# Filler products of ones in TensorE's waits at stage changes and at the end of the setup, inverses awaited in pairs, and a conditioning product placed ahead of the turned rows

## The reference, cut to what matters

```python
for l in range(DEPTH):                                   # DEPTH = 2
    mod = (silu(c) @ w_mod + b_mod).reshape(c.shape[0], 9, 1, 1024)
    h = modulate(rmsnorm(x, norm_w[0]), mod[:, 0], mod[:, 1])
    x = x + 0.5 * mod[:, 2] * swiglu(h, ffn1_w_in, ffn1_w_out)
    h = modulate(rmsnorm(x, norm_w[1]), mod[:, 3], mod[:, 4])
    mix, new = token_mixers(h, ...)                      # SSD, GLA and dilated attention, then w_out
    x = x + mod[:, 5] * mix
    h = modulate(rmsnorm(x, norm_w[2]), mod[:, 6], mod[:, 7])
    x = x + 0.5 * mod[:, 8] * swiglu(h, ffn2_w_in, ffn2_w_out)
y = rmsnorm(x, norm_f)
```

## Time and profile before

| | value |
|---|---|
| median of 3 runs | 2466.9 us (2463.86 to 2469.29) |
| the profiled execution, its time | 2464.18 us |
| its span, first to last instruction | 2461.3 us |
| mean granted TensorE clock | 0.992 |
| PE busy | 2399.5 us, 97% of the span |
| DVE busy | 1630.4 us, 66% |
| ACT busy | 1033.2 us, 42% |

### The profile page before, as it was taken

How to read it: one execution, slowest core, us unless ns; L and a number is a source line. 1 busy time by engine, 2 the same in 40 slices (tenths; PEclk the granted TensorE clock), 3 DMA queues, 4 the chain that set the end, 5 groups by cost and what they waited for, 6 DMA issues and landing times. The chain is left out here.

```text
span 2461.3 us, 48269 instructions
## 1 busy us (share of the span) xinstructions
PE 2399.5 (97%) x18967; PEld 2243.0 (91%) x18967; DVE 1630.4 (66%) x2800; ACT 1033.2 (42%) x1679; POOL 11.4 (0%) x43
## 2 busy tenths in 40 slices
PE   7999999999999999999999999999999999999998
PEld 5998999898977999899999999988999689999997
DVE  7872784565857786288478538736577678846854
ACT  5551452343554554145255315415256445523532
POOL 0000000000000000000000000000000000000000
PEclk8999999999999999999999999999999999999999
DMA  8246335622233224723233553364221431323331
GB/s 303 82 134 223 109 99 187 203 61 74 76 123 96 69 79 136 230 80 96 87 83 86 165 187 103 112 230 133 61 75 51 144 99 52 103 83 89 93 88 62
DMA packets 367530, 285.81 MB, mean 116 GB/s; under 512 B 18273, under 2 KB 355479, under 8 KB 366982
## 3 DMA queue, kind: packets, MB, share of 16 engines
q1 hardware_dynamic: 366956, 283.36, 37.3%
q10 hardware_dynamic: 410, 0.18, 0.0%
HBM read 271.71 MB, written 11.79 MB: 115 GB/s over the span
## 5 line engine op out<-in xcount | busy, mean ns | idle before, releaser
L352 PE MATMUL PS<-f_xH,f_wqH 128*128 128x288 f32 x2140 | 635.5, 297 | 3.1 <-issue 3.0
L352 PE MATMUL PS<-f_xL,f_wqH 128*128 128x288 f32 x2140 | 632.5, 296 | 0.0
L352 PE MATMUL PS<-f_xH,f_wqL 128*128 128x288 f32 x2140 | 630.5, 295 | 0.0
L352 PEld LDWEIGHTS PS<-f_xH,f_wqH 128*128 128x128 f32 x2140 | 401.4, 188 | 6.2 <-issue 5.6
L352 PEld LDWEIGHTS PS<-f_xH,f_wqL 128*128 128x128 f32 x2140 | 403.5, 189 | 0.0
L352 PEld LDWEIGHTS PS<-f_xL,f_wqH 128*128 128x128 f32 x2140 | 402.0, 188 | 0.0
L352 PE MATMUL PS<-f_actH,f_wqH 128*128 128x288 f32 x1408 | 321.5, 300 | 1.3 <-DVE f_wqL L1044 1.3
L352 PE MATMUL PS<-f_actH,f_wqL 128*128 128x288 f32 x1408 | 315.7, 296 | 0.0
L352 PE MATMUL PS<-f_actL,f_wqH 128*128 128x288 f32 x1408 | 315.7, 296 | 0.0
L776 DVE SCALAR_TENSOR_TENSOR xT<-PS,modT,xT 128x288 f32<-128x288 f32 (+1 forms) x80 | 41.4, 517 | 361.6 <-PE PS L352 361.4
L352 PEld LDWEIGHTS PS<-f_actH,f_wqH 128*128 128x128 f32 x1408 | 230.8, 189 | 27.0 <-issue 25.0
(11 more groups left out here) (541 smaller groups left out, 4274.0 us busy)
## 6 DMA issues: line engine op xcount, KB each, us to landing
wslot<-in_ffn_w_in SPq DMA_DIRECT2D x176, 512.0 KB, 5.0
masks<-in_w_mod SPq DMA_DIRECT2D x42, 1536.0 KB, 6.5
wslot<-in_ffn_w_out SPq DMA_DIRECT2D x64, 384.0 KB, 4.2
wslot<-in_w_in SPq DMA_DIRECT2D x48, 512.0 KB, 4.8
wslot<-in_ffn_w_out SPq DMA_DIRECT2D x64, 320.0 KB, 3.4
setup<-in_w_mod SPq DMA_DIRECT2D x6, 1536.0 KB, 12.9
wslot<-in_w_out SPq DMA_DIRECT2D x16, 512.0 KB, 4.6
dec<-in_cache_attn_k SPq DMA_DIRECT2D x16, 384.0 KB, 3.9
```

The lines of the kernel that those rows point to most:

```text
L352: ins = e.matmul(outs[j], w, x_hl[j][part], start=(start and w is wh and part == 0), stop=(stop and w is wl), skip_group_check=True)
```

## The change

Eight edits, all on TensorE's stream. Fillers are products of the constant tile `ones` (128 x 128, float32) with itself, into a PSUM bank that nobody reads; they signal nothing and wait for nothing. They stand: ten behind the last `turn_rows` of the setup; six behind the last down product of each of the four feed-forward blocks; three ahead of the last `values` of each attention part and four at that block's end; five at the end of each output projection. In the output projection `part(2)` waits for two of ACT's four copies and `part(3)` for all four. In the setup `products_of(5)` moves ahead of the turns of groups 0 to 3.

```diff
@@ setup, TensorE
-                for m in range(4):
+                products_of(5)
+                for m in range(5):
                     turn_rows(m)
-                products_of(5)
-                turn_rows(4)
                 turn_rows(5).then_inc(sem("mods_turned"), 1)
+                for _ in range(10):
+                    e.matmul(PS[:, 1, 0:P], ones[:], ones[:], start=True, stop=True)
@@ new helper
+        def warm(e, bank, n):
+            for _ in range(n):
+                e.matmul(PS[:, bank, 0:P], ones[:], ones[:], start=True, stop=True, skip_group_check=True)
@@ ffn_block, TensorE
                             for h in range(2):
                                 for d in range(DT - 2, DT):
                                     last_down(d, h)
+                            warm(e, 1, 6)
@@ input projection and attention, TensorE
+                        if s - 4 == NU - 2:
+                            warm(e, 4, 3)
                         if 0 <= s - 4 < NU and s % 2 == 0:
                             values(s - 4)
                         if 0 <= s - 2 < NU:
                             turn(s - 2)
                         if s == CIN_TURN:
                             turn_cin()
+                    warm(e, 4, 4)
@@ output projection, TensorE
                     spread_inverses()
-                    e.wait_ge(sem("y_spread_kept"), 2 * SG)
                     for d in range(2, 4):
+                        e.wait_ge(sem("y_spread_kept"), 2 * (d - 1))
                         part(d, READY)
@@ end of the output projection, TensorE
                     for h in range(2):
                         for d in range(DT - 2, DT):
                             last_part(d, h)
+                    warm(e, out_bank(4), 5)
```

## The result

The changed kernel takes 2477.15 us at the median of 20 executions (2467.61 to 2484.88), against 2466.49 us for 20 of the kernel before (2461.46 to 2472.39). The ratio is 1.0035, with a 95% interval of 1.0025 to 1.0044. So the change costs 0.35%, 8.6 us by the ratio (10.7 between the two medians), where I had forecast no change.

A forecast was written before the change was run, and what follows sets the result against it. TensorE, busy 97% of the span, was taken as the bound, leaving its pauses, clock and work. Terms 5.2 - 0.3 + 1.6 - 1.8 - 4.6 = +0.1 us, plus 0.4, made 2466.9 + 0.5 = 2467.4 us, range 2462 to 2472.

The forecast's parts named there:

- attention: Attention's end, twice: meeting 0.3 us later, 1.2 us of clock gained; net -0.9 us each, -1.8 in all.
- the inverses: Inverses awaited in pairs, twice: 0.6 us earlier start plus 1.7 us of clock; -2.3 us each, -4.6 in all.
- I take -1.2: Clock gain per layer behind attention's end, where the slow stretch would run at full clock; bounds 0 and -1.6 us.
- so that gives the full 1.7 us: Clock gain per layer behind the inverses: the clock holds after the pause falls from 1.44 to 0.85 us.
- the difference between executions: Whole kernel: in other executions the clock falls at other pauses, so fewer twofold gains; 0.4 us added.
- Feed-forward ends: Four ends, six fillers each ahead of the meeting: +1.31 us each, +5.2 in all, less 0.3 of clock.
- Rival 1: Drain does not wait for the fillers, so the meetings are not held up: 2459 us, chance 0.13.
- The gain of -0.3: Feed-forward ends: full clock at the input projection's opening saves 0.3 us once; bounds 0 and -1.7.
- Setup: Ten fillers at the setup's end cost 2.6 us, a warm first stage returns 1.0, moved product 0: +1.6.
- the bound: Setup: most the first stage could gain from a full clock, -1.9 us, half of its first 3.8 us.
- Output projection's end: Five fillers (1.09 us) end before DVE's last sum: 0, at most +0.1 us.
- rival 2: The clock falls anyway, a little later, behind unshortened real pauses; fillers are paid, little returns: 2474 us, chance 0.13.

The follow-up runs named there:

- e12: The kernel before, unchanged, run again for a second profile: 2468.17 us (12 executions), ratio 1.0000 [0.9989, 1.0011].
- e14: The kernel before, unchanged, run for a third profile: one execution, 2467.62 us.
- e1: The whole change again, against the kernel before: 2477.43 us (8 executions), ratio 1.0035 [1.0022, 1.0048].
- e5: Only the six fillers at each feed-forward end added to the kernel before: 2473.35 us (12 executions), ratio 1.0024 [1.0011, 1.0037].
- e11: Only fillers at each feed-forward end, twelve instead of six, added to the kernel before: 2476.24 us (7 executions), ratio 1.0046 [1.0028, 1.0064].
- e8: Only the fillers at attention's end and the output projection's end added to the kernel before: 2473.11 us (12 executions), ratio 1.0017 [1.0001, 1.0033].
- e9: Only the three and four fillers at attention's end added to the kernel before: 2470.33 us (12 executions), ratio 1.0010 [0.9999, 1.0022].
- e15: Only attention's fillers added to the kernel before, run again for a second profile: one execution, 2461.41 us.

## Why the prediction was wrong

**The parts add up.** By the ratios of the parts run alone: feed-forward ends +5.9, setup +1.2, attention +2.5, output end +0.2, pairs -2.0; together +7.8 us, against +8.6 for the whole. Each part is known to 2 or 3 us, so their sum to some 6: it calls for no hidden interaction, and can't exclude a small one. A second sum, from the traces, comes to the same: four ends of 1.31, the setup's 2.7 less 0.5, twice 0.53 at attention's end, and nothing gained in the state-space stages in the mean, +8.5. My terms were +4.9, +1.6, -1.8, 0 and -4.6 (of which the pairs are all of the last). The miss therefore lies mostly in two terms: attention, off by 4.3 us, and the inverses, off by 2.6.

**The step that failed** is the gain of clock in these two, "I take -1.2" and "so that gives the full 1.7 us". The mechanism was seen right in the profile after: both pauses shrank (that at the inverses to 0.86 us, for 0.85 worked out), the clock held at both places, and the stages took 131.0 and 131.1 us against 133.3 and 133.7, which is -2.3 and -2.6, where I had -1.2 - 2.3 = -3.5 in each. Over all profiles of the two kernels it is 134.5 against 134.5: of the 7 us forecast for the two stages nothing is left in the mean. What was wrong was to take one execution's falls for the kernel's. The execution that I read had its falls in the state-space stages exactly at the two places that the change touches. e12 and e14 show that the same kernel also falls some 60 and 75 us into the stage, at work that the change leaves alone, and in such a stage the early falls may be missing, so that there is nothing to save. After the change such falls are still there (e1: 0.94 and 0.91 over the stages), and the mean clock is 0.990 or 0.991 in both kernels. I had named the difference between executions and set it at 0.4 us; by the two terms it was worth some 7. The smaller error in the same term is the delay at attention's end, 0.53 us a layer for 0.3.

**Feed-forward ends.** Right, and the best-founded part: 1.32 us for 1.31 forecast, the same at all four ends, pause unchanged. e5 and e11 show that the price is linear. Rival 1, that the meeting isn't held up, is excluded. This hangs on the drain, and the sentence of the Trainium skill weighed in the prediction (PSUM — Partial Sum Buffer, "Engine vs sequencer instructions") agrees with the trace: with six more products in the queue the report came 1.32 us later. By that rule alone one would have rejected this part of the change. The gain of -0.3 there did not come: with the fillers ahead of the meeting the clock fell behind these ends no less often than without.

**Setup.** Right in kind and size: fillers at half clock, DVE 2.7 us later for 2.6 forecast, 0.5 us back in the first stage where I had 1.0. Two numbers of that paragraph were wrong without weight in the sum: 0.3 + 1.0 is 1.3 and not 1.2, and the opening ran at half clock for its first 4.7 us, not 3.8, so the bound is -2.3 and not -1.9. Moving the product was free by the rows, as worked out; it was not run without the fillers. The two edits together measured +1.2 us.

**Output projection's end.** Right: 0.

**The rivals.** The outcome is near rival 2, slower by unreturned clock: I had it at 2474 with 0.13. Its mechanism holds at the feed-forward ends, where the clock falls behind the real pause with the fillers as without. In the state-space stages it was another: the clock did not fall again behind attention's end or the inverses; it fell elsewhere, where it had fallen before as well.

**What stays open.** Whether attention's fillers cost more than their delay of 1.1 us. e8 and e9 measured 4 and 2.5 us, but both intervals hold 1.1; their mean clock of 0.989 speaks for more falls, and e15's single profile speaks against a rule. Why the clock falls at one place in one execution and at another in the next isn't shown by any run either. Nor does a run isolate the narrow products and transposes as the cause of the falls 60 us into the stage: fillers among them weren't tried.

## What to carry to other kernels

A filler has to stand where the engine waits for others, not where others wait for it: ask who reports last at the meeting, and put it behind the meeting if it is this engine. A clock's falls read from one profiled execution are a sample; before they are entered in a sum, look at several profiles of the same kernel, or compare the mean clock over many executions. And where a fall is avoided at one place, check the mean clock, not that place.

## What the runs showed of the hardware

The same program's executions differ by up to 17 us (2467.61 to 2484.88) with their clock: in the changed kernel 0.993 to 0.995 at 2468 us and 0.987 to 0.989 over 2480 us. Stretches at half clock in the state-space stages lasted 3.4, 6.8 or 10.2 us and cost there about 0.41 us per us: 131.0 us with 3.4 us at half, 136.6 with 17.1, 139.4 with 23.9.

The clock fell behind a pause of 1.44 us (the inverses, kernel before) and behind one of 2.21 us (layer 0's second feed-forward end, changed kernel) in one execution and not in another of the same kernel. It also fell in the middle of work that counts as busy: at 765.9 us in e12 amid products over 8 columns and transposes, and at 37.6 us in the first profile of before, behind 24 products over 9 columns and amid the 16 of `products_of(5)`, without a pause. Products of ones in float32 ran at half clock for 4.0 us in the setup before the clock rose at 46.8.
